# Differential attention's norm: root from ScalarE's logarithm and exponential with one Newton step, and the whole combination of short heads on GpSimd

## The reference, cut to what matters

```python
def diff_attention(q, k, v, lam_params, g_norm, lambda_init):
    ...
    def block(inp):
        ...
        s = jnp.einsum('ibhqd,ibhkd->ibhqk', qblk, kh) + bias
        p = jax.nn.softmax(s, axis=-1)
        a = p[0] - lam * p[1]
        return jnp.einsum('bhqk,bhkv->bhqv', a, vh)
    o = lax.map(block, (qb, starts))
    o = o.transpose(1, 2, 0, 3, 4).reshape(B, H, T, DIFF_DV)
    o = rmsnorm(o, g_norm) * (1.0 - lambda_init)
```

## Time and profile before

| what | value |
|---|---|
| median of 3 runs | 3385.5 us (3385.05, 3385.5, 3393.41) |
| the profiled execution | 3387.87 us |
| its span | 3386.1 us |
| PE busy | 3268.4 us, 97% |
| DVE, ACT, POOL busy | 2010.2, 1329.7, 1097.9 us |
| mean granted TensorE clock | 0.985 |
| differential attention | about 2014 to 2708 us of the span |

### The profile page before, as it was taken

One profiled execution on the slowest core, in us unless ns is written; L12 is line 12 of the kernel. 1 busy time (PEld: TensorE's weight loads), 2 busy tenths in 40 slices (PEclk: granted clock), 3 DMA queues, 4 the chain that ended last, 5 costly groups with the idle time before them and its releaser, 6 DMA issues. The chain is left out here.

```text
span 3386.1 us, 50920 instructions
## 1 busy us (share of the span) xinstructions
PE 3268.4 (97%) x19012; PEld 2552.1 (75%) x19012; DVE 2010.2 (59%) x4623; ACT 1329.7 (39%) x2170; POOL 1097.9 (32%) x511
## 2 busy tenths in 40 slices
PE   7999999998999999999999988999999888999998
PEld 6888888887888888888877765666666566888887
DVE  3322312226667666676667778888888466556654
ACT  3111111114334343444322336666666565333322
POOL 2412313243333333333333325555555433000000
PEclk9999999999999999999999989999999999999999
DMA  6545445465454544544459964122121366667562
GB/s 210 191 147 185 166 153 182 167 216 182 135 191 138 186 149 132 193 137 148 138 168 298 323 209 146 38 78 77 53 63 38 106 236 220 235 225 240 174 219 73
DMA packets 319013, 555.62 MB, mean 164 GB/s; under 512 B 35694, under 2 KB 115438, under 8 KB 318768
## 3 DMA queue, kind: packets, MB, share of 16 engines
q1 hardware_dynamic: 267296, 471.66, 42.9%
q10 hardware_dynamic: 51472, 80.71, 6.6%
HBM read 382.43 MB, written 169.82 MB: 163 GB/s over the span
## 5 line engine op out<-in xcount | busy, mean ns | idle before, releaser
L774 POOL TENSOR_TENSOR glaf_w_lo<-early_raw,glaf_w_hi 128x1024 fp32r<-128x1024 f32 x140 | 342.9, 2450 | 631.0 <-ACT glaf_w_hi L748 629.4
L803 PE MATMUL glaf_dense_acc<-h_hi,glaf_w_hi 128*128 128x512 f32 x1120 | 451.3, 403 | 5.5 <-ACT glaf_dense_out L757 4.1
L803 PE MATMUL glaf_dense_acc<-h_lo,glaf_w_hi 128*128 128x512 f32 x1120 | 439.3, 392 | 0.0
L803 PE MATMUL glaf_dense_acc<-h_hi,glaf_w_lo 128*128 128x512 f32 x1120 | 436.5, 391 | 0.0
L1792 DVE CUSTOM_DVE_ANT_0 front_p<-diff_s_ps,ahead_table 128x512 f32<-128x512 f32 x544 | 347.2, 687 | 72.4 <-PE diff_s_ps L1654 71.6
L555 POOL TENSOR_TENSOR proj_w_lo<-early_raw,proj_w_hi 128x1024 fp32r<-128x1024 f32 x84 | 202.8, 2415 | 481.7 <-DVE proj_w_hi L505 481.7
L1735 ACT ACTIVATE front_p<-front_p,diff_neg_max 128x2048 f32<-128x2048 f32 (+1 forms) x160 | 278.8, 1743 | 7.1 <-DVE diff_neg_max L1800 7.0
L1678 PE MATMUL diff_oT_ps<-diff_aT,diff_v 128*128 128x512 f32 x544 | 272.4, 602 | 4.7 <-ACT diff_aT L1729 4.7
L215 PE MATMUL proj_acc<-h_hi,proj_w_hi 128*128 128x512 f32 x672 | 263.0, 391 | 0.6 <-POOL proj_w_lo L555 0.6
L1653 PE MATMUL diff_s_ps<-ahead_k,ahead_q_high 128*128 128x512 f32 x544 | 244.6, 450 | 18.4 <-PEq L75 8.7
L217 PE MATMUL proj_acc<-h_hi,proj_w_lo 128*128 128x512 f32 x672 | 261.7, 389 | 0.0
(11 more groups left out here) (223 smaller groups left out, 7158.8 us busy)
## 6 DMA issues: line engine op xcount, KB each, us to landing
early_raw<-in_w_zg SPq DMA_DIRECT2D x180, 512.0 KB, 4.2
early_raw<-in_w_stream SPq DMA_DIRECT2D x80, 512.0 KB, 3.6
scratch_zg<-glaf_dense_out SPq DMA_DIRECT2D x140, 256.0 KB, 2.2
items_raw<-in_w_br SPq DMA_DIRECT2D x120, 256.0 KB, 2.9
merge_gate<-scratch_zg SPq DMA_DIRECT2D x120, 256.0 KB, 3.4
scratch_featT<-proj_out ACTq DMA_DIRECT2D x80, 256.0 KB, 2.3
items_br_hi<-scratch_item_hi SPq DMA_DIRECT2D x60, 256.0 KB, 6.1
items_br_lo<-scratch_item_lo SPq DMA_DIRECT2D x60, 256.0 KB, 6.4
```

The lines of the kernel that those rows point to most:

```text
L774: pool.tensor_tensor(self.w_lo[:, s], self.raw[:, u % self.RAW], self.w_hi[:, s], ALU.subtract).then_inc(self.lo_split, 1)
L803: done = pe.matmul(self.acc[:, u % self.banks], a, x, start=i == 0, stop=i == self.PER - 1)
```

## The change

There are two parts. In short heads (turns 0 to 15, `SHORT`) GpSimd makes the whole combination, all 512 keys, and VectorE stops after `ratio`; those who waited for `near_done` of a short turn wait for `far_done`. And the inverse root is no longer made by DVE alone: DVE makes the variance, ACT takes its logarithm and the exponential of minus half of that (`root`), and DVE makes one Newton step of three instructions (`refine`). `root` stands in ACT's list between the second evacuation and the second exponential of the closing turn, `refine` in DVE's list after the closing turn's maximum. ACT's table set is now the one that holds both functions.

```diff
+        variance, newton = (n_ps[:, i * G:(i + 1) * G] for i in range(1, 3))
...
-        NORM_STEPS = 2 + RSQRT_STEPS
+        NORM_STEPS = 5
+        SHORT = G * first_group[[T for _, T, _ in heads].index(TMAX)]
...
             def far(o):
-                half = slice(o.T // 2, o.T)
+                half = slice(o.T // 2 if o.n >= SHORT else 0, o.T)
...
-                if o.quarter == 0 and c == 0:
-                    pe.wait_ge(near_done, G * (o.g + 1))
-                if 2 * kt >= o.nk - 1:
+                short = G * o.g < SHORT
+                if o.quarter == 0 and c == 0 and not short:
+                    pe.wait_ge(near_done, G * (o.g + 1) - SHORT)
+                if short or 2 * kt >= o.nk - 1:
                     pe.wait_ge(far_done, G * (o.g + 1))
...
-            act.preload_act_table(ACT.Exp)
+            act.preload_act_table_set("natural_log_exp_and_others")
...
+            def root(g):
+                act.wait_ge(norm_steps, g * NORM_STEPS + 2)
+                act.activation(stat[:, 1], variance, ACT.Ln).then_inc(root_steps, 1)
+                act.wait_ge(root_steps, 2 * g + 1)
+                act.activation(stat[:, 1], stat[:, 1], ACT.Exp, scale=-0.5).then_inc(root_steps, 1)
...
                 if ku > 1:
                     evacuate(o, 1)
+                if g is not None:
+                    root(g)
                 if e:
                     exponentials(e, 1)
...
+                if o.n < SHORT:
+                    return
                 if o.g >= 2:
                     dve.wait_ge(turned, chunks_before[o.g - 1])
                 dve.scalar_tensor_tensor(a[:, o.g % 2, o.j, near], ...
...
-                var, tmp = (n_ps[:, i * G:(i + 1) * G] for i in range(1, 3))
-                step(dve.scalar_tensor_tensor(var, n_ps[:, 0:G], 1.0 / P, stat[:, 0], ALU.mult, ALU.add))
-                rsqrt_by_psum(step, dve, stat[:, 2], var, tmp)
+                dve.scalar_tensor_tensor(variance, n_ps[:, 0:G], 1.0 / P, stat[:, 0], ALU.mult, ALU.add).then_inc(norm_steps, 1)
+
+            def refine(g):
+                step = Chain(dve, norm_steps, g * NORM_STEPS + 2)
+                dve.wait_ge(root_steps, 2 * g + 2)
+                step(dve.scalar_tensor_tensor(newton, variance, -0.5, stat[:, 1], ALU.mult, ALU.mult))
+                step(dve.tensor_tensor(newton, newton, stat[:, 1], ALU.mult))
+                dve.scalar_tensor_tensor(stat[:, 2], newton, 1.5, stat[:, 1], ALU.add, ALU.mult).then_inc(norm_steps, 1)
...
                 if n.live:
                     maximum(n)
+                if closing(t) is not None:
+                    refine(closing(t))
```

More of the change, by code:

```diff
@@ L1492, in phase_diff @@
         norm_steps = m.sem("norm_steps")
+        root_steps = m.sem("root_steps")
         diag_ready = m.sem("diag_ready")
@@ L1599, in _ @@
             load_z(NG - 1)
-            sp.wait_ge(near_done, TURNS)
+            sp.wait_ge(near_done, TURNS - SHORT)
             sp.wait_ge(far_done, TURNS)
@@ L1786, in bias_max @@
                 if c == 0 and n.n >= SLOTS:
-                    dve.wait_ge(near_done, n.n - SLOTS + 1)
+                    if n.n - SLOTS >= SHORT:
+                        dve.wait_ge(near_done, n.n - SLOTS + 1 - SHORT)
                     dve.wait_ge(far_done, n.n - SLOTS + 1)
```

## The result

| what | before | after |
|---|---|---|
| median of 9 runs each | 3388.94 us | 3398.59 us |
| ratio after to before, 95% interval | | 1.0033 [1.0023, 1.0043] |
| span of the profiled execution | 3386.1 us | 3397.3 us |
| mean granted clock | 0.985 | 0.985 |

The forecast was 3400 us, 14.3 us or 0.42% more. The ratio says 0.33%, 11.2 us, and the two profiled spans differ by 11.2 us too; the two medians lie 9.7 us apart.

What follows compares the result with a forecast made beforehand. TensorE bounds long heads, DVE the stretch from 2076 to 2108, and a chain through unfilled engines the short heads. 10.1 - 1.1 - 0.9 + 6.2 = 14.3 us on 3385.5 gives 3400 us; range 3387 to 3409 us.

Steps and rivals of the forecast that it cites:

- 1.24 us for the scale: Short heads, POOL: scale of 512 elements, by a straight line from 0.748 us (256) at 1.91 ns an element.
- Some 0.1 us less if it runs without DVE's combination beside it: Short heads, POOL: allowance on the 1.24 us scale of 512 elements when DVE's combination doesn't run beside it.
- the faster rival: Short heads: DVE is the bound, POOL hides behind it, needing under 1.9 us a turn; 3381 us, chance 0.10.
- 1.0 us for the clock: Short heads: longer TensorE waits at joints mean more time at 1.2 GHz; 1.0 us, from 0 to 3.
- the forecast of 9.2 us up to joint 5: Short heads, up to the first long group's transposes: 10.1 us of losses, with 0.9 us less for group 1's spread.
- 15 x 0.41 us: Long-head closings: root ahead of ACT's second exponential delays evacuation and PE by 0.41 us in 15 closings, 6.2 us.
- The rival with slack: Long-head closings: evacuation has slack, so the two small activations are hidden; 3393.6 us, chance 0.17 together with cheap scale.
- 1.1 us less at the end: Last closing, alone on the path: the shorter root brings the diagonal after its variance 1.1 us sooner.
- 0.9 us less for group 1's spread: Short heads: group 1's spread waits 1.22 us for the norm's diagonal; the shorter root saves 0.9 us.
- DVE's long combination: Closings: it waits up to 0.4 us beside POOL's diagonal, 0.3 taken, felt only where DVE is the bound.

Runs made afterwards that it cites:

- scale alone: Kernel before, with DVE's combination waiting until POOL's scale of the same turn is done; 3670.28 us in one execution.
- with products: Overwritten extra TensorE products added in short heads to late-root, late-table kernels: joint 5 at 89.07 us (combination shared) and 95.74 us (GpSimd alone).
- the last kernel: Whole change plus root behind the last evacuation, extra TensorE products and far bias table loaded late; ratio to before 1.0000 [0.9991, 1.0008].
- root only: Changed kernel with SHORT = 0: only the new root, short heads combined as before; ratio to before 1.0006 [0.9997, 1.0015].
- root only, late, table late: New root alone, behind the last evacuation in long closings, far bias table loaded after group 2's queries; ratio to before 0.9994 [0.9984, 1.0003].
- before with the table late: Kernel before with the far bias table loaded after group 2's queries, nothing else; ratio to before 1.0000 [0.9991, 1.0009].
- root only, late: New root alone (SHORT = 0), placed behind the last evacuation of long closing turns; ratio to before 0.9986 [0.9976, 0.9997].
- short heads only: Kernel before with GpSimd's whole combination in short heads and the old root; ratio to before 1.0026 [1.0011, 1.0041].

## Why the prediction was right, and where its terms were not

**Right in direction, in the places, and in who waits for whom; two sizes were wrong.** The time went where the sum had put it: into the joints of the short heads and into ACT's list among long heads. POOL is the releaser of all four joints, long groups grew, the tables were loaded once. The total was 3 us too high; in the profiled execution 2.2 of them lay in the phases ahead, which the change doesn't touch, 0.6 in the phase and 0.3 behind it.

**The term "1.24 us for the scale" failed.** It measured 0.69 us. The line through two sizes had both its points taken beside a DVE instruction whose length grows with the same size, so its slope of 1.91 ns an element was the slope of two engines sharing, not of POOL. "Some 0.1 us less if it runs without DVE's combination beside it" was the step to doubt: "scale alone" gives 0.27 us less at 256 and 1.09 at 1024. By the Trainium skill, "GPSIMD Engine Reference", section "Engine selection", one-input work on GpSimd runs roughly at line rate; the trace agrees, 0.84 ns an element. The prediction had set this aside because of its row, but the row held something else. With 2.06 us a combination in the prediction's own sums, the joints would have come 0.8 us later for group 0 (2.5 predicted, 0.79 measured), 2.25 - 3 x 0.43 = 0.95 for group 1 (measured 0.98), 3.05 - 2 x 0.43 = 2.2 for group 2. Together that is 3.9 us less than forecast. The joints of groups 2 and 3, which stand behind a low clock, moved by more, 3.6 and 3.4 us. The 2.06 us still exceed the 1.9 us that the prediction had estimated for a turn of DVE without its combination, so the faster rival, whose condition was under 1.9 us, did not come about.

**The term "1.0 us for the clock" failed the other way.** Without the scale's excess and the clock, the forecast of 9.2 us up to joint 5 would have been 4.3, or 5.2 if the shorter root gives nothing back there (below); 9.7 were measured, which leaves 4.5 to 5.4 for the clock. The two windows shown with the result say the same directly: PE is busy 5.2 us longer with the same 279 records. The experiments say it in another way. With the root late in all four kernels:

| joint 5 | combination shared | GpSimd alone | difference |
|---|---|---|---|
| no products | 91.88 | 103.77 | 11.9 |
| with products | 89.07 | 95.74 | 6.7 |

5.2 us of the difference vanish when PE is given work in its waits. (In the upper right one the table is still early, but its scores don't wait for their queries at turn 8; in the lower left one there are fewer products, 6 instead of 11. With the root early on the right side, the products bring 6.6 us against 2.8, a difference of 3.8. Each number is one execution.) The prediction had seen the waits of 3 us and taken 1.0 us for the clock, at most 3; there were three stretches at 1.2 GHz instead of one behind joints 2 to 4, and in them PE was nearly full, so they counted almost whole. The remaining 6.7 us are more than the 5.2 us of the corrected terms (4.3 and the 0.9 of the root); the last kernel still shows a clock near 0.5 at 18 to 20 us from the first score matmul, which its counterpart doesn't, but that this is the other 1.5 us was not tested.

So two errors of about 4 us stood against each other, and the sum was right for the short heads (9.2 against 9.7) by luck. A reader should take the mechanism from it, not the agreement.

**"15 x 0.41 us" for ACT held,** as 15 x 0.37 = 5.5 us. The rival with slack is ruled out: the delay of 0.38 us at the exponential arrived at PE as 0.35. Moving the same instructions behind the evacuations removed all of it.

**"1.1 us less at the end" held.** The last diagonal came 1.17 us sooner behind its variance. From joint 5 to the last gate the kernel took 4.0 us more, which with 5.5 us of ACT leaves -1.5; in the six kernels with the late root the way from joint 5 to the last gate was 1.1 to 1.4 us shorter than before.

**"0.9 us less for group 1's spread"** holds for the wait itself as long as short heads stay as they were: PE's wait for that diagonal went from 1.22 us in before to 0.17 in "root only" and in "root only, late, table late". Joint 5 came 1.4 us earlier in the first and 1.1 in the second (against before with the table late), but 1.6 later in "root only, late". With GpSimd's whole combination the term is nothing: in "short heads only", which has the old long root, that spread doesn't wait for its diagonal at all, since PE's work ahead of it already runs late. So the term should not have been taken off the change. That after is even 1.9 us behind "short heads only" is open: the two differ in the clock up to joint 5 (0.85 and 0.87), but "short heads only" has one profiled execution, and 1.9 us is within the spread of two executions of one program.

**DVE's long combination** beside the diagonal stretched: its mean rose from 1286 to 1401 ns over 64, with a longest of 1778 ns, so up to 0.5 us in a closing where 0.3 had been taken. Among long heads it fell on a DVE that had time.

## What to carry to other kernels

Of an instruction that slows beside another engine's work, two sizes in a trace give no price if both ran beside that work: look at what stood beside each, or measure it alone. Where a chain hands work between engines, the price of a slower link can be its delay plus what PE then does at 1.2 GHz; here the second was about as large as the first (5.2 us of longer busy PE, 4.5 of longer idle PE), and filling PE's waits with products of no use took most of it away. And a small instruction costs by its place in the list, not its length: 0.4 us on ACT cost 5.5 us of the kernel ahead of an evacuation, and nothing measurable two instructions further down. Last, run one program twice before a difference of 2 or 3 us inside one stage is given a cause: here two executions of the same instructions lay 3.0 us apart.

## What the runs showed of the hardware

- GpSimd's scale takes 0.84 ns an element without DVE's combination beside it (482 ns for 256, 693 for 512, 1127 for 1024), and nearly twice that, 2215 ns for 1024, beside a DVE instruction with two SBUF inputs. The Trainium skill, "GPSIMD Engine Reference", section "Key points", has the contention; its size is in these rows: the scale grew by 1.09 us beside a combination of 1.29 us, and DVE's combination grew by 2.17 us beside an addition of 2.37 us.
- The clock behind a joint: 1.2 GHz behind idle times of 3.15 and 1.69 us (joints 3 and 4 after), 2.4 GHz behind 0.93 us and none (the same joints before). The idle time right ahead does not order it alone: before joint 2 it was 1.02 us in before, and behind that the clock of 2045 to 2049 was 0.57.
- A logarithm and an exponential of 128x4 took 173 and 205 ns, 0.32 us from the start of the first to the start of what stood behind the second.
- A transfer that had been hidden came to be waited for: up to 2.6 us at turn 8 (3.5 with the products), with the queries queued behind a table that nobody needs before turn 16. Their arrival moved by 2 us between executions (24.5 us or less from the first score in before, 26.5 in "root only, late"), more than PE's start did (0.6 us).
